# Output projection as a stage of its own, with the second norm's squares and sums between its columns

## The chip, the core and the metric

One Trainium2 chip, one core of it. The kernel is one program of 74 thousand instructions on five engines: TensorE (PE, with its weight loads shown apart as PEld), VectorE (DVE), ScalarE (ACT), GpSimd (POOL) and SyncE (SP, which issues the DMAs here). The metric is the device time of one execution in microseconds; lower is better. Runs of the same kernel differ by up to 4 us here.

## The reference

Two layers of a diffusion backbone over 640 tokens (512 latent, 128 context) of width 1024. What matters for the change is the middle of a layer:

```python
y, k_new, v_new, s_rwkv, s_lru = token_mixers(h, lp, ...)   # ends in concat([a, b, c]) @ lp['w_out']
x = x + g1 * y                                              # gated residual
h2 = rmsnorm(x, lp['norm2_g']) * (1.0 + sc2) + sh2          # x * rsqrt(mean(x*x) + eps) * g
x = x + g2 * peer_ffn(h2, ...)                              # begins with q = h2 @ peer_wq  (1024 x 2048)
```

So x has 1024 features for each token, and the second norm needs for each token the sum of 1024 squares of the x that the output projection has just updated.

## The kernel before

Features lie on the 128 partitions, tokens in the free dimension: `g.xT` is [128, 8, 640], eight chunks (KC = 8) of 128 features. All products are in float32 quality: an operand is split in a high and a low part of type float32r, and `split3` (L197 to L201) issues three matmuls for each product, of 320 columns each (half of the 640 tokens, so that a result of 640 tokens takes two PSUM banks).

`gemm` (L209) is one block that does a whole product of this kind; the output projection (8 output columns of 128 features, called "wout") and the query projection (16 columns, "query") are two calls of it. In it SP issues the weight chunks (512 KB each, a ring of R = 4), ACT rounds each to its high part (`high`, L242), DVE makes the low part (`low`, L293), PE runs a column of 2 halves x 8 chunks x 3 matmuls = 48 matmuls in one PSUM bank pair (R = 4 pairs, all eight banks), and DVE takes the sums. For wout, `take` is the gated residual in place on `g.xT` (L1538, three instructions: tokens 0 to 319, 320 to 511, 512 to 639). The first two columns (SR = 2) go chunk by chunk through the right-hand side, as its parts become ready; from then on a column is done at a time. High and low parts have two slots, so column n + 2 is rounded once column n is done.

A block begins and ends with a barrier of all engines; after wout there is also a block that clears the semaphores (`g.end`, L127). SP too issues nothing of the next block before that.

`norm_programs` (L435) gives a norm as parts that `gemm` puts ahead of its own work:

- `scalar_first`: ACT squares the eight chunks of xT (L448, 128x640 each).
- `tensor`: PE sums the squares over partitions, a matmul with an all-ones matrix in plain float32, for each chunk one of 512 and one of 128 columns (L471). The profile counts two instructions for each such float32 matmul (x32 for 16).
- `vector`: DVE turns the sums into mean plus epsilon (L476), then waits for the root, scales chunk by chunk (L486) and makes the low parts (L481).
- `scalar`: ACT computes the root as Ln (L453) and Exp (L455), each after a table load, then applies gain and shift (L460, two instructions for a chunk) and rounds to the high part (L465).

In the query block the order on each engine is thus:

- SP: `prefetch` (the keys `kt`, 1 MB; four chunks `u` of 512 KB), then the ring of four query weight chunks, then the rest as slots come free.
- ACT: squares 0 to 7, `high(0)`, `high(1)`, root, chunks of the norm, further `high`.
- PE: sums of the squares, then columns 0 and 1 chunk by chunk, then the rest.
- DVE: `low(0)`, `low(1)`, mean, (root), scaling and low parts of the norm, then takes and `low` in turn.

The same `norm_programs` serves the first norm of a layer and the final norm; for them the change leaves the order as it is. Everything from the end of the query block on (selection, gates, experts, fold) is later blocks that start one after the other.

Of the kernel before, what the change touches and what calls it, by code (L numbers as in the profile page):

```python
# [25 lines left out]
F32 = mybir.dt.float32  # L26
U32 = mybir.dt.uint32
F32R = mybir.dt.float32r
BF16 = mybir.dt.bfloat16
ALU = mybir.AluOpType  # L30
ACT = mybir.ActivationFunctionType
AX = mybir.AxisListType

P = 128
D = 1024
DEPTH = 2
NS = 512
NPR = 128
NT = NS + NPR
# [3 lines left out]
KC = D // P  # L43
# [13 lines left out]
RMS_EPS = 1e-6  # L57
# [139 lines left out]
def split3(pe, out, lhs, rhs, start=True, stop=True):  # L197

    pe.matmul(out, lhs[1], rhs[0], start=start, stop=False)  # L199
    pe.matmul(out, lhs[0], rhs[1], start=False, stop=False)  # L200
    return pe.matmul(out, lhs[0], rhs[0], start=False, stop=stop)  # L201
# [230 lines left out]
    c.then(ve.tensor_tensor(g.gain[:, i, :, :], g.gain[:, i, :, :], v(name).unsqueeze(2).broadcast_to([P, KC, 2]), ALU.mult))  # L432


def norm_programs(g, st, name, out, gain, shift, squares, low=None, kept=None, roots=None, chunks=None):  # L435

    nc = g.nc
    sq_ready, sum_ready, r_ready, steps = (g.sem(f"{name}_{x}") for x in ("squared", "summed", "root", "steps"))  # L440
    log_ready, scaled, normed, lowed = (g.sem(f"{name}_{x}") for x in ("log", "scaled", "normed", "low"))
    rs = g.sb(st, "rs", [P, 2, NT]) if roots is None else roots
    t = chunks
    raw = (lambda kc: out[:, kc, :]) if low is None else (lambda kc: t[:, kc % 3, :]) if kept is None else (lambda kc: kept[:, kc, :])

    def scalar_first(act):
        for kc in range(KC):
            nc.scalar.activation(squares[:, kc, :], g.xT[:, kc, :], ACT.Square).then_inc(sq_ready, 1)  # L448

    def scalar(act):  # L450
        act.wait_ge(steps, 1)

        nc.scalar.activation(rs[:, 1, :], rs[:, 0, :], ACT.Ln).then_inc(log_ready, 1)  # L453
        act.wait_ge(log_ready, 1)
        nc.scalar.activation(rs[:, 0, :], rs[:, 1, :], ACT.Exp, scale=-0.5).then_inc(r_ready, 1)  # L455

        for kc in range(KC):
            act.wait_ge(scaled, kc + 1)
            for c, (a, b) in enumerate(((0, NS), (NS, NT))):
                last = nc.scalar.activation(raw(kc)[:, a:b], raw(kc)[:, a:b], ACT.Identity,  # L460
                                            scale=gain(kc, c), bias=shift(kc, c) if shift else 0.0)
            last.then_inc(normed, 1)
            if low is not None:
                act.wait_ge(normed, 2 * kc + 1)
                nc.scalar.activation(out[:, kc, :], raw(kc), ACT.Copy).then_inc(normed, 1)  # L465

    def tensor(pe):
        for kc in range(KC):
            pe.wait_ge(sq_ready, kc + 1)
            for bank, (a, b) in enumerate(((0, NS), (NS, NT))):  # L470
                mm = pe.matmul(g.ps[:, bank, 0:b - a], g.ones, squares[:, kc, a:b], start=(kc == 0), stop=(kc == KC - 1))  # L471
            mm.then_inc(sum_ready, 1)
    def vector(ve):
        c = Counter(ve, steps)
        ve.wait_ge(sum_ready, KC)
        c.did(ve.tensor_scalar(rs[:, 0, :], g.flat[:, 0:NT], 1.0 / D, RMS_EPS, ALU.mult, ALU.add))  # L476
        ve.wait_ge(r_ready, 1)

        def lower(kc):
            ve.wait_ge(normed, 2 * kc + 2)  # L480
            ve.tensor_tensor(low[:, kc, :], raw(kc), out[:, kc, :].bitcast(F32), ALU.subtract).then_inc(lowed, 1)  # L481

        for kc in range(KC):
            if low is not None and kept is None and kc >= 3:
                ve.wait_ge(lowed, kc - 2)
            ve.tensor_tensor(raw(kc), g.xT[:, kc, :], rs[:, 0, :], ALU.mult).then_inc(scaled, 1)  # L486
            if low is not None and kc >= 1:
                lower(kc - 1)
        if low is not None:
            lower(KC - 1)  # L490

    return {"scalar_first": scalar_first, "scalar": scalar, "tensor": tensor, "vector_first": lambda ve: None, "vector": vector,
            "chunk_low": lowed}


# [1036 lines left out]
def residual_take(g, part):  # L1532

    def take(ve, oc, sums):
        for a, b in ((0, H2), (H2, NS), (NS, NT)):
            c, h = int(a >= NS), a // H2
            x = g.xT[:, bass.ds(oc, 1), a:b]
            i = ve.scalar_tensor_tensor(x, sums[:, h:h + 1, a - h * H2:b - h * H2], g.modT[:, bass.ds(part * KC + oc, 1), c], x,  # L1538
                                        ALU.mult, ALU.add)
        return i  # L1540
    return take


AHEAD = 64
IN_SELECT = 52
U_RING = 4
# [321 lines left out]
H2 = NT // 2  # L1868
# [479 lines left out]
def build(nc, dram):  # L2348
    ctx = ExitStack()
    with ctx:  # L2350
# [25 lines left out]
        with nc.Fori(0, DEPTH) as l:  # L2376
            g.begin()
            with ExitStack() as s1:
                g.proj = g.sb(s1, "proj", [P, NPROJ + 1, NT])
                g.vtok = g.sb(s1, "vtok", [P, TILES, VTOK])  # L2380
                with ExitStack() as s2:
                    g.h2 = [g.sb(s2, f"h{x}", [P, KC, NT], F32R) for x in ("hi", "lo")]
                    proj_stage(g, l)
                g.outT = g.sb(s1, "outT", [P, KC, NT])
                with ExitStack() as s2:
                    g.kctx = g.sb(s2, "kctx", [P, CB, PAST])
                    g.vctx = g.sb(s2, "vctx", [P, PAST // P, 512])
                    keep = (g.sb(s2, "ar", [P, 2, CA, TILES, 2, P]), g.sb(s2, "gt", [P, CA, NT]), g.sb(s2, "pc", [P, 2, CA, NT // CH]))
                    with ExitStack() as s3:
                        mod = Modulation(g, s3, lambda i: dram["mod_late"][l, i], g.modL, MODS_FIRST, 4)  # L2390
                        rwkv_prepare(g, l, keep, mod)
                    mix_stage(g, l, keep)
                    mix_finish(g, l, keep)
                with ExitStack() as s2:
                    out2 = [g.sb(s2, f"out{x}", [P, KC, NT], F32R) for x in ("hi", "lo")]
                    gemm(g, "wout", lambda oc: dram["w_out"][l, oc], KC, 4, 2, out2, residual_take(g, 2),
                         lambda st: split_programs(g, "out", g.outT, *out2))
            g.end()
            g.begin()
            with ExitStack() as s1:  # L2400
                h = g.sb(s1, "h", [P, KC, NT])
                hid = HiddenAhead(g, s1, l, h)
                own = Gathered(g, s1)
                with ExitStack() as s2:
                    sel = g.sb(s2, "sel", [P, 3, NT])
                    with ExitStack() as s3:
                        kt = g.sb(s3, "kt", [P, 2 * PH, P])
                        keys_loaded = g.sem("sel_keys_loaded")
                        qT = g.sb(s3, "qT", [P, 2 * PH, NT])

                        def prefetch(sync):
                            sync.dma_start(kt[:, :, :], dram["peer_keys"][l]).then_inc(keys_loaded, 16)
                            for n in range(U_RING):
                                hid.load(sync, n, n, first=True)

                        with ExitStack() as s4:
                            h2 = [g.sb(s4, f"h{x}", [P, KC, NT], F32R) for x in ("hi", "lo")]
                            gemm(g, "query", lambda oc: dram["peer_wq"][l, oc], 2 * PH, 4, 2, h2,
                                 lambda ve, oc, sums: ve.tensor_copy(qT[:, bass.ds(oc, 1), :].rearrange("p o (h n) -> p (o h) n", n=H2), sums),
                                 lambda st: norm_programs(g, st, "norm2", h2[0], lambda kc, c: g.gain[:, 1, kc, c:c + 1],  # L2420
                                                          lambda kc, c: g.modT[:, 3 * KC + kc, c:c + 1], h, low=h2[1], kept=h,
                                                          roots=sel[:, 0:2, :]), prefetch)
                        select_stage(g, l, qT, sel, kt, keys_loaded, hid, own)
                    gates_stored = [g.sem(f"gate_stored{i}") for i in range(2)]
                    gates_stage(g, l, sel, hid, gates_stored, own)
                experts_stage(g, l, hid, gates_stored, own)
                fold_stage(g, own.acc)
            g.end()

        g.begin()  # L2430
        with ExitStack() as s1:
            out = g.sb(s1, "out", [P, KC, NT])
            with ExitStack() as s2, nc.Block() as block:  # L2433
                final = norm_programs(g, s2, "final", out, lambda kc, c: g.v("final", kc, kc + 1), None, out)
                @block.scalar
                def _(act):
                    final["scalar_first"](act)
                    final["scalar"](act)
# [121 lines left out]
```

## Time and profile before

| | us |
|---|---|
| median of 3 runs | 4712.85 (4710.88 to 4714.87) |
| profiled execution | 4709.56 |
| its span | 4707.8 |
| PE busy | 4159.8 (88%) |
| DVE busy | 3554.3 (75%) |
| ACT busy | 1493.6 (32%) |

Engines are busy side by side, so the shares say little on one stage; a stage is read by which engine, wait or transfer ends last there. Each of the two layers has one wout block and one query block: wout from 747.5 to 817.0 us and from 3060.9 to 3130.4, query following from 818.25 and 3131.71. In a timeline a row is: start, length, engine, line, operation, output <- inputs, shape, count of merged instructions, and in brackets how long the engine idled before and what released it.

### The profile page before, as it was taken

Reading aid. Unit: us, or ns where it says so; the run is one execution under the profiler, and the core shown is the slowest. Engines: PE = TensorE matmul, PEld = TensorE weight load, DVE = VectorE, ACT = ScalarE, POOL = GpSimd, SP = SyncE. Lnnn points to the kernel's source line nnn. Section 1 sums busy time; section 2 is a strip of 40 time slices with the busy share of each in tenths; the row PEclk is TensorE's granted clock in tenths of the full one; section 3 lists DMA queues with packets and bytes.
Section 4 is the critical chain, followed back from the end, with each engine's and each line's share of the span. In section 5 each row is a group of like instructions: output and inputs, shape, how many; then the busy total and the mean of one; then the engine's idle time right before and its main releaser. Section 6 shows DMA issues by size and latency. Waiting matters only on the chain. (4 is left out here: it accounts for less than half of the span.)

```text
span 4707.8 us, 73952 instructions
## 1 busy us (share of the span) xinstructions
PE 4159.8 (88%) x28014; PEld 3384.9 (72%) x28014; DVE 3554.3 (75%) x6633; ACT 1493.6 (32%) x2210; POOL 1329.6 (28%) x1046
## 2 busy tenths in 40 slices
PE   7979987899698999999889799879987889999996
PEld 5957776865476887878779477579654678888875
DVE  3456643379997999999955566433899989999997
ACT  4424523211133333332252455231111332333333
POOL 0000000013303665666500000000332056566663
PEclk8978878999899999999999789789998999999998
DMA  6230002258779999999821300121786899999995
GB/s 234 63 115 2 2 2 105 85 182 308 258 205 326 409 409 408 404 406 404 331 90 41 115 2 2 56 98 52 274 287 204 242 388 409 409 405 407 403 406 222
DMA packets 408295, 1079.48 MB, mean 229 GB/s; under 512 B 37728, under 2 KB 183392, under 8 KB 401376
## 3 DMA queue, kind: packets, MB, share of 16 engines
q1 hardware_dynamic: 260576, 539.10, 32.3%
q0 software_dynamic: 147456, 536.94, 29.5%
q8 instruction: 157, 2.57, 0.2%
q14 instruction: 106, 0.87, 0.1%
HBM read 996.47 MB, written 79.43 MB: 229 GB/s over the span
## 5 line engine op out<-in xcount | busy, mean ns | idle before, releaser
L1618 POOL DMA_INDIRECT ring<-peer_u_rows,rows x512 | 625.7, 1222 | 2439.8 <-DVEq L1859 1512.8
L1618 POOL DMA_INDIRECT ring<-peer_v,rows x512 | 679.3, 1327 | 405.2 <-DVE acc L2252 336.1
L199 PE MATMUL ps<-vhi,wlo 128*128 128x512 f32 x1536 | 618.9, 403 | 134.8 <-DVE wlo L2231 133.1
L1575 PE MATMUL ps<-h,u 128*128 128x384 f32 x2048 | 689.0, 495 | 27.0 <-ACT hh L1586 25.0
L2252 DVE SCALAR_TENSOR_TENSOR acc<-ring,act,acc 128x1024 f32<-128x1024 f32 x508 | 647.3, 1281 | 45.8 <-DMA ring<-peer_v,rows 39.0
L1622 DVE SCALAR_TENSOR_TENSOR ring<-ring,acc 128x1024 f32<-128x1024 f32 x512 | 623.7, 1224 | 36.0 <-DMA ring<-peer_u_rows,rows 29.1
L200 PE MATMUL ps<-vlo,whi 128*128 128x512 f32 x1536 | 613.4, 399 | 0.0
L201 PE MATMUL ps<-vhi,whi 128*128 128x512 f32 x1536 | 612.9, 399 | 0.0
L1575 PEld LDWEIGHTS ps<-h,u 128*128 128x128 f32 x2048 | 390.2, 193 | 289.5 <-issue 42.9
L199 PEld LDWEIGHTS ps<-vhi,wlo 128*128 128x128 f32 x1536 | 297.7, 194 | 215.6 <-issue 142.0
L199 PE MATMUL ps<-xhi,ulo 128*128 128x384 f32 x1024 | 344.5, 336 | 18.6 <-DVE xlo L2209 18.6
L201 PE MATMUL ps<-xhi,uhi 128*128 128x384 f32 x1024 | 344.3, 336 | 0.0
L200 PE MATMUL ps<-xlo,uhi 128*128 128x384 f32 x1024 | 343.9, 336 | 0.0
L201 PEld LDWEIGHTS ps<-vhi,whi 128*128 128x128 f32 x1536 | 297.5, 194 | 64.3
L200 PEld LDWEIGHTS ps<-vlo,whi 128*128 128x128 f32 x1536 | 297.6, 194 | 61.5
L2217 DVE TENSOR_TENSOR vlo<-v,vhi 128x1024 fp32r<-128x1024 f32 x256 | 312.4, 1220 | 24.2 <-ACT vhi L2161 24.2
L2161 ACT ACTIVATE vhi<-v 128x1024 fp32r<-128x1024 f32 x256 | 269.6, 1053 | 169.2 <-DMA v<-peer_v 161.8
L2166 ACT ACTIVATE whi<-u 128x384 fp32r<-128x384 f32 x128 | 66.8, 523 | 682.8 <-DVE u L2226 682.8
L1586 ACT ACTIVATE hh<-ps 128x384 f32<-128x384 f32 x256 | 122.6, 481 | 424.0 <-PE ps L1575 391.5
L199 PE MATMUL ps<-hhi,proj_lo 128*128 128x320 f32 x672 | 210.5, 313 | 15.2 <-DVE hlo L481 15.2
L200 PE MATMUL ps<-hlo,proj_hi 128*128 128x320 f32 x672 | 208.8, 311 | 0.0
L199 PEld LDWEIGHTS ps<-xhi,ulo 128*128 128x128 f32 x1024 | 193.4, 189 | 21.4 <-DVE xlo L2209 19.0
(356 smaller groups left out, 8054.2 us busy)
## 6 DMA issues: line engine op xcount, KB each, us to landing
u<-peer_u SPq DMA_DIRECT2D x256, 512.0 KB
v<-peer_v SPq DMA_DIRECT2D x256, 512.0 KB
gates<-stage SPq DMA_DIRECT2D x24, 2048.0 KB, 9.6
gw<-gates SPq DMA_DIRECT2D x64, 768.0 KB
mod_ring<-mod_late SPq DMA_DIRECT2D x32, 1024.0 KB, 7.6
hidden<-hh SPq DMA_DIRECT2D x128, 192.0 KB
u<-hidden SPq DMA_DIRECT2D x128, 192.0 KB
proj_raw<-w_proj SPq DMA_DIRECT2D x42, 512.0 KB, 3.7
```

The source lines that it names most:

```text
L199: pe.matmul(out, lhs[1], rhs[0], start=start, stop=False)
L200: pe.matmul(out, lhs[0], rhs[1], start=False, stop=False)
L201: return pe.matmul(out, lhs[0], rhs[0], start=False, stop=stop)
L1575: mm = pe.matmul(self.g.ps[:, bank, 0:ND], self.u[:, slot, kc, :], self.x[:, kc, 0:ND], start=(kc == 0), stop=(kc == KC - 1))
L1586: return self.g.nc.scalar.activation(self.hh[:, slot, :], self.g.ps[:, slot, 0:ND], ACT.Gelu)
L1618: return pool.indirect_dma_start(to, None, table, rows)
L1622: return ve.scalar_tensor_tensor(row, row, 1.0, self.acc[:, x, :], ALU.mult, ALU.mult, accum_out=self.act[x][:, slot:slot + 1])
L2161: nc.scalar.activation(v2[0][:, j, :], v[:, j % 2, :], ACT.Copy).then_inc(v_hi, 1)
L2166: nc.scalar.activation(w2[0][:, j, :], h, ACT.Copy).then_inc(w_hi, 1)
L2217: ve.tensor_tensor(v2[1][:, j, :], v[:, j % 2, :], v2[0][:, j, :].bitcast(F32), ALU.subtract).then_inc(v_lo, 1)
L2252: ve.scalar_tensor_tensor(acc, r, w, acc, ALU.mult, ALU.add).then_inc(used, 1)
```

## The change

- `wout_stage` replaces the call of `gemm` for wout. It has the same columns, splits and residual, written out without loops: three PSUM bank pairs for the columns (`R`), banks 6 and 7 for the sums of squares. ACT squares a chunk of xT once DVE has updated it (`square`), behind the `high` of a later column, in a buffer of two chunks. PE sums the squares of column n - 2 behind column n (`squares`), those of columns 6 and 7 at the end.
- `norm_programs` takes `summed`, the place of finished sums in PSUM. With it, ACT squares nothing and PE sums nothing in the query block; DVE forms the mean as its first instruction (`vector_first`) and ACT the root as its first (`scalar_first`), both ahead of the query's weights.

```diff
-def norm_programs(g, st, name, out, gain, shift, squares, low=None, kept=None, roots=None, chunks=None):
+def norm_programs(g, st, name, out, gain, shift, squares, low=None, kept=None, roots=None, chunks=None, summed=None):
@@ -443,16 +443,22 @@
...
-    def scalar_first(act):
-        for kc in range(KC):
-            nc.scalar.activation(squares[:, kc, :], g.xT[:, kc, :], ACT.Square).then_inc(sq_ready, 1)
-
-    def scalar(act):
+    def root(act):
         act.wait_ge(steps, 1)
-
         nc.scalar.activation(rs[:, 1, :], rs[:, 0, :], ACT.Ln).then_inc(log_ready, 1)
         act.wait_ge(log_ready, 1)
         nc.scalar.activation(rs[:, 0, :], rs[:, 1, :], ACT.Exp, scale=-0.5).then_inc(r_ready, 1)
+    def scalar_first(act):
+        if summed is not None:
+            root(act)
+            return
+        for kc in range(KC):
+            nc.scalar.activation(squares[:, kc, :], g.xT[:, kc, :], ACT.Square).then_inc(sq_ready, 1)
+    def scalar(act):
+        if summed is None:
+            root(act)
...
     def tensor(pe):
-        for kc in range(KC):
+        for kc in range(KC) if summed is None else ():
             pe.wait_ge(sq_ready, kc + 1)
             for bank, (a, b) in enumerate(((0, NS), (NS, NT))):
                 mm = pe.matmul(g.ps[:, bank, 0:b - a], g.ones, squares[:, kc, a:b], start=(kc == 0), stop=(kc == KC - 1))
             mm.then_inc(sum_ready, 1)
+    def mean(ve):
+        at = 0 if summed is None else summed
+        ve.tensor_scalar(rs[:, 0, :], g.flat[:, at:at + NT], 1.0 / D, RMS_EPS, ALU.mult, ALU.add).then_inc(steps, 1)
     def vector(ve):
-        c = Counter(ve, steps)
-        ve.wait_ge(sum_ready, KC)
-        c.did(ve.tensor_scalar(rs[:, 0, :], g.flat[:, 0:NT], 1.0 / D, RMS_EPS, ALU.mult, ALU.add))
+        if summed is None:
+            ve.wait_ge(sum_ready, KC)
+            mean(ve)
         ve.wait_ge(r_ready, 1)
         def lower(kc):
@@ -489,7 +499,7 @@
         if low is not None:
             lower(KC - 1)
-    return {"scalar_first": scalar_first, "scalar": scalar, "tensor": tensor, "vector_first": lambda ve: None, "vector": vector,
+    return {"scalar_first": scalar_first, "scalar": scalar, "tensor": tensor, "vector_first": (lambda ve: None) if summed is None else mean, "vector": vector,
             "chunk_low": lowed}
@@ -1541,6 +1551,108 @@
     return take
+def wout_stage(g, l):
+    nc, d = g.nc, g.dram
+    R, S, W = 3, 2, 4
+    w_in = [g.sem(f"wout_w_loaded{i}") for i in range(W)]
+    w_hi, w_lo, ready, taken = (g.sem(f"wout_{x}") for x in ("w_high", "w_low", "sums_ready", "sums_taken"))
+    squared, summed = g.sem("norm2_squared"), g.sem("norm2_summed")
+    take = residual_take(g, 2)
+    with ExitStack() as st, nc.Block() as block:
+        out2 = [g.sb(st, f"out{x}", [P, KC, NT], F32R) for x in ("hi", "lo")]
+        parts = split_programs(g, "out", g.outT, *out2)
+        raw = g.sb(st, "wout_raw", [P, W, KC, P])
+        hi = g.sb(st, "wout_hi", [P, S, KC, P], F32R)
+        lo = g.sb(st, "wout_lo", [P, S, KC, P], F32R)
+        sq = g.sb(st, "sq", [P, 2, NT])
+        @block.sync
+        def _(sync):
+            for n in range(KC):
+                if n >= W:
+                    sync.wait_ge(w_lo, n - W + 1)
+                sync.dma_start(raw[:, n % W, :, :], d["w_out"][l, n]).then_inc(w_in[n % W], 16)
+        @block.scalar
+        def _(act):
+            def high(n):
+                act.wait_ge(w_in[n % W], 16 * (n // W + 1))
+                if n >= S:
+                    act.wait_ge(ready, n - S + 1)
+                nc.scalar.activation(hi[:, n % S, :, :], raw[:, n % W, :, :], ACT.Copy).then_inc(w_hi, 1)
+            def square(n):
+                act.wait_ge(taken, n + 1)
+                if n >= 2:
+                    act.wait_ge(summed, n - 1)
+                nc.scalar.activation(sq[:, n % 2, :], g.xT[:, n, :], ACT.Square).then_inc(squared, 1)
+            parts["scalar_first"](act)
+            for n in range(S):
+                high(n)
+            parts["scalar"](act)
+            for n in range(KC):
+                if n + S < KC:
+                    high(n + S)
+                if n >= 1:
+                    square(n - 1)
+            square(KC - 1)
+        @block.tensor
+        def _(pe):
+            def chunk(n, h, kc):
+                w = (hi[:, n % S, kc, :], lo[:, n % S, kc, :])
+                return split3(pe, g.ps[:, 2 * (n % R) + h, 0:H2], w, [x[:, kc, h * H2:(h + 1) * H2] for x in out2],
+                              start=(kc == 0), stop=(kc == KC - 1))
+            def squares(n):
+                pe.wait_ge(squared, n + 1)
+                for bank, (a, b) in enumerate(((0, NS), (NS, NT))):
+                    mm = pe.matmul(g.ps[:, 2 * R + bank, 0:b - a], g.ones, sq[:, n % 2, a:b], start=(n == 0), stop=(n == KC - 1))
+                mm.then_inc(summed, 1)
+            pe.wait_ge(w_lo, S)
+            for kc in range(KC):
+                pe.wait_ge(parts["chunk_low"], kc + 1)
+                for n in range(S):
+                    for h in range(2):
+                        mm = chunk(n, h, kc)
+                    if kc == KC - 1:
+                        mm.then_inc(ready, 1)
+            for n in range(S, KC):
+                pe.wait_ge(w_lo, n + 1)
+                if n >= R:
+                    pe.wait_ge(taken, n - R + 1)
+                for h in range(2):
+                    for kc in range(KC):
+                        mm = chunk(n, h, kc)
+                mm.then_inc(ready, 1)
+                squares(n - 2)
+            squares(KC - 2)
+            squares(KC - 1)
+        @block.vector
+        def _(ve):
+            def low(n):
+                ve.wait_ge(w_hi, n + 1)
+                ve.tensor_tensor(lo[:, n % S, :, :], raw[:, n % W, :, :], hi[:, n % S, :, :].bitcast(F32), ALU.subtract).then_inc(w_lo, 1)
+            parts["vector_first"](ve)
+            for n in range(S):
+                low(n)
+            parts["vector"](ve)
+            for n in range(KC):
+                ve.wait_ge(ready, n + 1)
+                take(ve, n, g.ps[:, 2 * (n % R):2 * (n % R) + 2, 0:H2]).then_inc(taken, 1)
+                if n + S < KC:
+                    low(n + S)
...
                     mix_finish(g, l, keep)
-                with ExitStack() as s2:
-                    out2 = [g.sb(s2, f"out{x}", [P, KC, NT], F32R) for x in ("hi", "lo")]
-                    gemm(g, "wout", lambda oc: dram["w_out"][l, oc], KC, 4, 2, out2, residual_take(g, 2),
-                         lambda st: split_programs(g, "out", g.outT, *out2))
+                wout_stage(g, l)
...
                                  lambda st: norm_programs(g, st, "norm2", h2[0], lambda kc, c: g.gain[:, 1, kc, c:c + 1],
                                                           lambda kc, c: g.modT[:, 3 * KC + kc, c:c + 1], h, low=h2[1], kept=h,
-                                                          roots=sel[:, 0:2, :]), prefetch)
+                                                          roots=sel[:, 0:2, :], summed=6 * 512), prefetch)
```

## Rows read from the trace of the kernel before

**Rows 1.** Busy time, share of the span and instructions of TensorE, from the page.
```profile
PE 4159.8 (88%) x28014; PEld 3384.9 (72%) x28014; DVE 3554.3 (75%) x6633; ACT 1493.6 (32%) x2210; POOL 1329.6 (28%) x1046
```

**Rows 2.** Timeline of DVE, layer 1, takes of wout columns 2, 3 and 7.
```profile
780.65 1.14 DVE L1538 SCALAR_TENSOR_TENSOR xT<-ps,modT,xT 128x320 f32<-128x320 f32 x3 [5.22 <-PE ps L201]
...
787.69 1.13 DVE L1538 SCALAR_TENSOR_TENSOR xT<-ps,modT,xT 128x320 f32<-128x320 f32 x3 [4.66 <-PE ps L201]
...
815.85 1.14 DVE L1538 SCALAR_TENSOR_TENSOR xT<-ps,modT,xT 128x320 f32<-128x320 f32 x3 [5.91 <-PE ps L201]
```

**Rows 3.** Group of one matmul form, 745 to 860 us: busy us, mean ns, idle before.
```profile
L199 PE MATMUL ps<-outhi,wout_lo 128*128 128x320 f32 x128 | 40.6, 317 | 11.4 <-DVE wout_lo L293 11.4
```

**Rows 4.** Timeline, layer 1: PE's sums of squares, then the query's first matmul.
```profile
819.04 8.92 PE L471 MATMUL ps<-h,keep 128*128 128x512 f32 x32 [3.23 <-ACT h L448]
819.57 0.19 PEld L471 LDWEIGHTS ps<-h,keep 128*128 128x128 f32 x1 [0.24 <-issue]
...
820.65 0.19 PEld L471 LDWEIGHTS ps<-h,keep 128*128 128x128 f32 x1 [0.24 <-issue]
...
840.57 0.60 PE L199 MATMUL ps<-hhi,query_lo 128*128 128x320 f32 x1 [12.61 <-DVE hlo L481]
```

**Rows 5.** Timeline of ACT, layer 1, query block up to the root.
```profile
818.25 5.12 ACT L448 ACTIVATE h<-xT 128x640 f32<-128x640 f32 x8 [15.36 <-PEq L127]
829.57 1.06 ACT L242 ACTIVATE query_hi<-query_raw 128x1024 fp32r<-128x1024 f32 x1 [6.20 <-DMA query_raw<-peer_wq]
830.84 1.06 ACT L242 ACTIVATE query_hi<-query_raw 128x1024 fp32r<-128x1024 f32 x1 [0.21 <-DMA query_raw<-peer_wq]
...
834.67 1.28 ACT L455 ACT_TABLE_LOAD   x1
```

**Rows 6.** Timeline of DVE, layer 1, query block up to the first scaling.
```profile
830.66 2.49 DVE L293 TENSOR_TENSOR query_lo<-query_raw,query_hi 128x1024 fp32r<-128x1024 f32 x2 [13.68 <-ACT query_hi L242]
833.07 0.81 DVE L476 TENSOR_SCALAR sel<-ps 128x640 f32<-128x640 f32 x1
836.74 1.56 DVE L486 TENSOR_TENSOR h<-xT,sel 128x640 f32<-128x640 f32 x2 [2.85 <-ACT sel L455]
```

**Rows 7.** Windows of 2 us in the query block, layer 1: PE, PEld, DVE, ACT, POOL busy, PEclk, DMA share, GB/s.
```profile
820.00:822.00 2.00, 2.00 (x9) 1.21 (x8) 0.00 (x0) 2.00 (x4) 0.00 (x0) 1.00 0.91 381
...
828.00:830.00 2.00, 0.00 (x0) 0.00 (x0) 0.00 (x0) 0.43 (x1) 0.00 (x0) 1.00 1.01 406
```

**Rows 8.** Timeline, layer 1, wout block: ACT's first work, PE's first matmul.
```profile
747.47 2.62 ACT L503 ACTIVATE outhi<-outT 128x640 fp32r<-128x640 f32 x4 [1.25 <-PEq L1453]
...
755.77 0.63 PE L199 MATMUL ps<-outhi,wout_lo 128*128 128x320 f32 x1 [9.76 <-DVE wout_lo L293]
```

**Rows 9.** Timeline of SP, layer 1: first DMA of wout, first of query.
```profile
747.84 28.15 SPq L232 DMA_DIRECT2D wout_raw<-w_out  x8
818.37 0.33 SPq L2412 DMA_DIRECT2D kt<-peer_keys  x1
```

**Rows 10.** Timeline, layer 2, all engines: squares, sums, first rounding, first scaling.
```profile
3131.71 5.12 ACT L448 ACTIVATE h<-xT 128x640 f32<-128x640 f32 x8 [15.36 <-PEq L127]
...
3132.49 11.84 PE L471 MATMUL ps<-h,keep 128*128 128x512 f32 x32 [3.23 <-ACT h L448]
...
3143.03 1.06 ACT L242 ACTIVATE query_hi<-query_raw 128x1024 fp32r<-128x1024 f32 x1 [6.20 <-DMA query_raw<-peer_wq]
...
3150.22 1.56 DVE L486 TENSOR_TENSOR h<-xT,sel 128x640 f32<-128x640 f32 x2 [2.85 <-ACT sel L455]
```

**Rows 11.** Windows around two entries of PE into a product; columns as in Rows 7.
```profile
757.00:759.00 2.00, 2.00 (x9) 2.00 (x9) 1.66 (x3) 0.00 (x0) 0.00 (x0) 0.50 0.79 215
759.00:761.00 2.00, 2.00 (x15) 2.00 (x13) 0.00 (x0) 0.00 (x0) 0.00 (x0) 0.91 0.17 68
842.00:844.00 2.00, 2.00 (x9) 2.00 (x9) 1.70 (x3) 1.97 (x5) 0.00 (x0) 0.50 0.00 0
844.00:846.00 2.00, 2.00 (x13) 2.00 (x12) 1.70 (x4) 1.97 (x4) 0.00 (x0) 0.83 0.03 8
```

## The prediction

> **What bounds the kernel now.** I read the page's busy shares first, then the groups of the stretch the diff touches, then its timelines engine by engine, then windows for DMA and the clock. PE is busy 88% of the span [rows 1], but that averages stages with other limits; the two edited blocks of a layer have to be read one by one.
>
> In the wout block PE is the limit. DVE takes column 2 at 780.65, column 3 at 787.69 and column 7 at 815.85 [rows 2]: 7.04 us from one to the next, five times over (35.20 / 5 = 7.04 to column 7). A column is 48 matmuls, so they follow each other every 0.147 us, and PE waits in this block only at its start and once behind the first two columns: 11.4 us in the group's idle time [rows 3], of which 9.8 us lie before the first matmul [rows 8] and 1.6 us are that second wait. DVE idles 4.66 us before a take, ACT more. Whatever is put on PE between columns lengthens this block; what is put on ACT or DVE does not.
>
> In the query block the limit, up to PE's first matmul at 840.57, is the load of the first weights. The block starts at 818.25; ACT's first rounding waits for the DMA until 829.57, the second until 830.84 [rows 5], 11.32 and 12.59 us after the start. In layer 2 the first comes at 3143.03 against 3131.71, again 11.32 [rows 10]. SP first issues keys and four u chunks; the DMA engines are at 0.91 of their time in a window while PE and ACT work and at 1.01 in one when both are idle [rows 7], so they carry what they can. The squares (5.12 us of ACT from 818.25, rows 5) and PE's sums (8.92 us from 819.04 to 827.96, rows 4) lie wholly beside this load and end 1.6 us before it. In layer 2 the sums took 11.84 us, to 3144.33 [rows 10], longer because PE ran a part of them at 1.2 GHz, and the scaling still began at the same distance from the block's start: 3150.22 - 3131.71 = 18.51, against 836.74 - 818.25 = 18.49 in layer 1. So the squares and the sums cost nothing today. What is exposed behind the load is the root: DVE makes the two low parts from 830.66, then the mean at 833.07, and scales from 836.74 [rows 6]. Mean, Ln, a table load and Exp are the 3.67 us between.
>
> **The change, part by part**, per layer, against the profiled execution (4709.56 us; the median of the runs is 3.3 above it).
>
> *Root first: a gain of 3.67 us.* The mean, the root and both table loads move to the block's start, on DVE and ACT, which have nothing else until 829.57. They are a 0.81 us mean, two loads of 1.28 us and two activations, some 5 us in all, under 11 us of load; that cover holds with 6 us to spare. DVE then scales where the mean stood, at 833.07 instead of 836.74 on the old time axis. ACT is free by then (its second rounding ends at 831.90). The norm's chunks follow at ACT's rhythm as before.
>
> The next sentences are by the way. In the trace the table load between Ln and Exp lasted 1.28 us and Exp came right behind it [rows 5]. The Trainium skill (ScalarE: Activation LUTs, "What ACT_TABLE_LOAD costs") puts a switch at 2.66 us, of which 1.38 are a drain. By it the exposed root would be 3.67 + 1.38 = 5.05 us and the net loss below 1.4 us smaller per layer. The timeline has no room for that drain, so the row decides.
>
> *Squares to ACT in wout: nothing.* Eight activations of 0.64 to 0.74 us (5.12 / 8 and one with its tail, rows 5), each behind a `high`, in a stage where ACT works about 1 us in 7. Only the last one is on the path, below. A square waits for the take of its column; the `high` queued behind it waits for a later column anyway, so nothing is held up.
>
> *Sums to PE between columns: a loss.* The weight loads of the sums repeat every 820.65 - 819.57 = 1.08 us for one chunk of 640 tokens at full clock [rows 4]. Five of them (chunks 0 to 4, behind columns 2 to 6) stand before the end of column 7. PE's other waits there are unchanged: the 1.6 us wait comes before column 2, the first sum only after it. So the last take starts at 815.85 + 5 x 1.08 = 821.25.
>
> *The new tail.* Before, the block's last work was the take, to 816.99. Now behind column 7, which ends for PE at about 821.05, come two more sums, to 823.21. Meanwhile the take ends at 822.39 and ACT's last square, 0.74 us and a handover, at 823.18. Then the last sum: 8.92 - 7 x 1.08 = 1.36 us with its drain, to 824.57. The block ends 824.57 - 816.99 = 7.6 us later. SP issues the query's loads only behind the barrier, so the whole 7.6 shifts the landing at 829.57 too. The bounds of this term: no more than 0 if PE had hidden waits for the sums; the price of a sum is 1.08 us at full clock and twice that at 1.2 GHz ((11.84 - 8.92) = 2.9 us more in layer 2), which I exclude because 0.147 us for a matmul is the high clock: at 1.2 GHz PE started only 9 in 2 us [rows 11]. What the trace doesn't show is a plain float32 matmul between float32r ones. From below it could overlap by the 0.15 us of one matmul; from above it could cost a fill on both sides, some 0.3 us by the 0.60 us of PE's first matmul against a mean of 0.317 [rows 3, 4]. I take 0, as PE goes through the sums' own switches between 512 and 128 columns without a gap.
>
> *Loops gone: a gain of 0.2 us.* SP's first DMA of wout comes 0.37 us after ACT's first work [rows 8, 9], that of the query, which has no loop ahead, 0.12 us after it [rows 5, 9]. The first weights gate PE's start, so 0.25 at most, 0 at least.
>
> *Clock.* PE enters wout and query at 0.50, 1.2 GHz, and leaves it within 3 to 5 us [rows 11]. It idled 9.8 and 12.6 us ahead of them [rows 4, 8]. After the change it will idle some 20 us ahead of the query and enter at the same level. Only how long it stays there may vary: 1.5 us more or less of low clock is 0.75 us per entry.
>
> *The sum*: +7.6 - 3.67 - 0.2 = +3.7 us per layer, +7.4 in both. Behind the query block everything starts in sequence and shifts along. Profiled: 4717.0 us. Runs: 4712.85 + 7.4 = 4720.3.
>
> **Rivals.**
>
> *Sums that cost more than their own time (slower).* Each is a switch of operand type, twice, in PE's stream. 16 sums carry it. My sum passes +0.2% (+9.4 us, about what a measurement here can tell from no change) once the extra is over (9.4 - 7.4) / 16 = 0.13 us each. At the upper bound of 0.3 us it is +4.8: 4725. A barrier that takes longer when PE's matmul is last, and low clock at the wrong place, add to the same side. For it: no row shows such a mixture. Against: no gap in PE's own sums.
>
> *Sums that are free (the norm's front simply shortens).* If PE had room between columns, only the tail would be left: behind the take's end a square and the last sum, 0.79 + 1.36 = +2.1, and -3.67 - 0.2, so -1.8 per layer, 4709.3. For it: the group's 11.4 us idle of PE [rows 3]. Against: none of them lies behind column 2's start, and the takes are evenly 7.04 apart.
>
> *The load is faster once nobody else works.* Squares and sums read SBUF during the load. Were the landing 2 us earlier, each layer would gain 2: 4716, and with free sums 4705. Against: 0.91 with PE and ACT at work, 1.01 without; and layer 2 landed after the same 11.32 us with sums 2.9 us longer.
>
> **How the numbers follow.** My case, with each term inside its bounds: 0.62, 4716 to 4722. Costlier sums or barrier: 0.25, above 4722.3, mostly below 4728. Free sums: 0.08, around 4709. Faster load: 0.05. Only the last two together go below 4703.4, 0.04 of it all. So faster 0.04, slower 0.25, within 0.2% 0.71. The range 4715.5 to 4727.5 leaves out the free sums and a little at the top.
>
> **What would show it.** Takes of columns 3 to 7 spaced 8.12 us instead of 7.04; the wout block 7.6 us longer from its first work to the next block's; no L448 and L471 in the query block; the first rounding still 11.3 us behind its start, the scaling 14.8 instead of 18.5; PE's first query matmul at 18.6 instead of 22.3 us. It would be wrong if takes are 7.1 or over 8.3 us apart, or if the first rounding comes at another distance.

## Result and profile after

| | before | after |
|---|---|---|
| median of 20 runs each | 4712.52 us | 4722.52 us (4712.21 to 4731.24) |
| ratio, 95% interval | | 1.0020 [1.0014, 1.0026] |
| the same pair once more (35 and 12 runs) | 4713.32 us | 4718.27 us, 1.0012 [1.0002, 1.0021] |
| span of the profiled execution | 4707.8 us | 4729.4 us |

The forecast was 4720.3 us. The first pair came out 10.0 us slower, the second 5.0; the forecast was 7.4. The two profiled executions lie 21.6 us apart, most of it (15.2 us) in a stage that the change doesn't touch, so the trace has to be read by stretches.

DVE in layer 1, the takes of columns 2, 3 and 7 and then its first work of the query block, answers to [rows 2, 6]:

```profile
788.86 1.14 DVE L1548 SCALAR_TENSOR_TENSOR xT<-ps,modT,xT 128x320 f32<-128x320 f32 x3 [5.22 <-PE ps L201]
...
796.98 1.14 DVE L1548 SCALAR_TENSOR_TENSOR xT<-ps,modT,xT 128x320 f32<-128x320 f32 x3 [5.75 <-PE ps L201]
...
829.46 1.14 DVE L1548 SCALAR_TENSOR_TENSOR xT<-ps,modT,xT 128x320 f32<-128x320 f32 x3 [6.99 <-PE ps L201]
834.08 0.82 DVE L481 TENSOR_SCALAR sel<-ps 128x640 f32<-128x640 f32 x1 [3.49 <-PEq L127]
846.73 2.50 DVE L293 TENSOR_TENSOR query_lo<-query_raw,query_hi 128x1024 fp32r<-128x1024 f32 x2 [11.82 <-ACT query_hi L242]
849.14 1.55 DVE L496 TENSOR_TENSOR h<-xT,sel 128x640 f32<-128x640 f32 x2
```

The takes are 8.12 us apart instead of 7.04, in layer 2 as well. The mean stands alone at the block's start, and the scaling follows the low parts at once, without the 2.85 us wait of [rows 6]. The end of the output projection, all engines (weight loads left out):

```profile
829.26 3.50 PE L1616 MATMUL ps<-sq,keep 128*128 128x512 f32 x12
829.46 1.14 DVE L1548 SCALAR_TENSOR_TENSOR xT<-ps,modT,xT 128x320 f32<-128x320 f32 x3 [6.99 <-PE ps L201]
...
830.63 0.74 ACT L1593 ACTIVATE sq<-xT 128x640 f32<-128x640 f32 x1 [7.38 <-DVE xT L1548]
...
834.02 1.28 ACT L448 ACT_TABLE_LOAD   x1 [2.65 <-PEq L127]
```

The last three sums run to 832.76, 3.30 us behind the start of the last take. ACT begins the next block 1.26 us later, as long as the barrier took behind the take before (816.99 to 818.25). ACT's part of the query block, answers to [rows 5]:

```profile
835.31 0.74 ACT L448 ACTIVATE sel<-sel 128x640 f32<-128x640 f32 x1
836.07 1.28 ACT L450 ACT_TABLE_LOAD   x1
837.36 0.74 ACT L450 ACTIVATE sel<-sel 128x640 f32<-128x640 f32 x1
845.64 1.06 ACT L242 ACTIVATE query_hi<-query_raw 128x1024 fp32r<-128x1024 f32 x1 [7.54 <-DMA query_raw<-peer_wq]
```

The root is done at 838.10, and ACT then waits 7.54 us for the weights. They land 11.5 us behind SP's first DMA of the block (834.16) in this layer and 11.3 in the other; before it was 11.2.

From such rows, by the first work of each stretch (us; M is the mixing stage ahead, from the store of the new keys to the output projection; "edited" runs from ACT's first work in the output projection to the query's first take, DVE's `qT` copy):

| kernel | M, layer 1 / 2 | edited, layer 1 / 2 | edited, sum against before (217.4) | median against before |
|---|---|---|---|---|
| before | 418.0 / 421.0 | 108.5 / 108.9 | | |
| before, again | 426.9 / 427.3 | 109.0 / 108.3 | | -0.3 |
| after | 427.9 / 426.3 | 111.7 / 112.7 | +7.1 | +10.0 |
| after, again | 420.8 / 421.0 | 112.5 / 112.6 | +7.7 | +5.0 |
| stage only | 424.6 / 424.3 | 108.8 / 108.7 | +0.1 | +0.5 |
| one sum | 427.5 / 420.8 | 107.6 / 108.5 | -1.3 | -0.9 |
| before, weights first | 428.2 / 416.7 | 103.4 / 106.1 | -7.8 | -4.4 |
| after, weights first | 417.9 / 420.5 | 104.9 / 104.9 | -7.5 | -4.7 |
| three sums | 420.4 / 419.8 | 107.8 / 106.8 | -2.8 | -4.1 |
| four sums, weights first | 427.4 / 421.3 | 104.3 / 103.6 | -9.4 | -4.9 |

(217.4 is the mean of the two profiles of the kernel before. Medians are against that of the kernel before in runs taken alongside: 4712.52 for the first row of after, 4713.32 down to "one sum", 4711.52 for the last four.)

What is left of the span beside M and the edited stretches takes 3648 to 3653 us in all ten profiles, without an order by kernel. From the query's first take to the end of the query block it is 102.3 us in both layers of every one. So what an edited stretch loses or gains isn't taken back later.

### The profile page after: what moved, and what is told of

Its sections match the earlier page's. It is cut to its first block and busy times, and to the rows that moved or that the text cites. A ratio compares the mean times of both kernels' runs of the same rounds, so it can differ in the third digit from the quotient of the medians.

```text
span 4729.4 us, 73908 instructions
## 1 busy us (share of the span) xinstructions
PE 4166.3 (88%) x28014; PEld 3397.1 (72%) x28014; DVE 3552.9 (75%) x6633; ACT 1494.3 (32%) x2210; POOL 1318.4 (28%) x1046
## 5 line engine op out<-in xcount | busy, mean ns | idle before, releaser
L1730 POOL DMA_INDIRECT ring<-peer_v,rows x512 | 660.5, 1290 | 424.0 <-DVE acc L2364 365.2
L199 PE MATMUL ps<-xhi,ulo 128*128 128x384 f32 x1024 | 344.4, 336 | 18.6 <-DVE xlo L2321 18.6
L199 PE MATMUL ps<-hhi,proj_lo 128*128 128x320 f32 x672 | 211.3, 314 | 16.3 <-DVE hlo L491 16.3
L201 PE MATMUL ps<-hhi,proj_hi 128*128 128x320 f32 x672 | 209.4, 312 | 0.0
```

The costliest lines, as they stand in the source:

```text
L1730: return pool.indirect_dma_start(to, None, table, rows)
```

## Experiments

**The same two kernels again.** No edit.

> The changed kernel once more, unaltered, for a second profile and more times. My theory: the change costs 3.2 to 3.8 us per layer in the two edited blocks (output projection 6.9 to 7.5 us longer from ACT's first work to the next block's first DMA, query 3.7 to 3.8 shorter up to its first take), 7 us in all, and the rest of the 10 us between the medians is the spread of the mixing stage, whose clock is uneven. It expects the same two differences again (70.9 to 78 us; 37.6 to 34 us), and the mixing stage of either layer anywhere from 416 to 430 us. Rival: the changed program makes the mixing stage itself slower. It expects 426 us or more again in both layers, against 418 and 421 before.

> The kernel before once more, unaltered, for a second profile of it. My theory (the mixing stage's time varies by itself): the mixing stage differs from 418.0 and 421.0 us by some us in either direction in at least one layer, the two edited blocks by less than 0.5 us (70.9 and 37.6). Rival (the changed program makes it slower): 418 to 421 us again in both layers. Ratio to the kernel before 1.000.

Measured: 4718.27 us (ratio 1.0012 [1.0002, 1.0021]) and 4713.07 us (0.9994 [0.9984, 1.0003]). Windows over M in the second profile of before and in the second of after, each layer a row (columns as in Rows 7):

```profile
329.50:756.40 426.90, 370.32 (x4905) 285.00 (x4904) 257.99 (x537) 175.63 (x370) 0.00 (x0) 0.80 0.06 23
2647.70:3075.00 427.30, 369.93 (x4904) 284.69 (x4896) 258.07 (x537) 175.54 (x370) 0.00 (x0) 0.80 0.07 23
```

```profile
329.60:750.40 420.80, 364.94 (x4908) 279.48 (x4907) 257.93 (x537) 175.18 (x371) 0.00 (x0) 0.81 0.07 23
2646.80:3067.70 420.90, 362.29 (x4908) 277.35 (x4907) 258.01 (x537) 175.34 (x370) 0.00 (x0) 0.82 0.07 23
```

With the same work of DVE and ACT, M takes 417 to 428 us in the ten profiles: the stretches over 426 us all have a mean granted clock of 0.80, the 416.7 of the kernel before with weights first has 0.83. PE runs the same matmuls in more busy time at the lower clock (370.32 against 364.94 and 362.29 us above). The rival (the changed program slows M) is out: before has it at 427 twice, after at 421 twice. The edited stretches repeat to within 0.8 us in a layer: in the second profile of the changed kernel the output projection takes 78.3 and 78.4 us, the query 34.3 and 34.2 to its first take.

**The stage alone, without squares.**

```diff
-    roots=sel[:, 0:2, :], summed=6 * 512), prefetch)
+    roots=sel[:, 0:2, :]), prefetch)
...
-                if n >= 1:
-                    square(n - 1)
-            square(KC - 1)
...
-                squares(n - 2)
-            squares(KC - 2)
-            squares(KC - 1)
```

> The output projection as a stage of its own without loops, with three pairs of banks, but without any square or sum in it; the second norm squares and sums in the query block as before, and its root stands behind the weights as before. My theory: only the loop's start goes, so the output projection takes 70.2 to 70.7 us instead of 70.9, query stays at 37.6 us to its first take, and the total is 0.4 to 1.4 us below the kernel before (4711 to 4712 if that is at 4712.5). Rival (the new stage itself, its written-out code or fewer banks, costs time): output projection over 71.5 us or total over 4716.

Measured: 4713.85 us, 1.0001 [0.9990, 1.0011]; the output projection takes 70.7 us in both layers (before: 70.9 twice, then 71.0 and 70.5), the query 38.0 us to its first take. The total didn't fall by the expected 0.4 to 1.4 us; a gain of that size can't be seen in these medians. SP's first DMA now stands 0.10 us behind ACT's first work instead of 0.36, but what that saves up to the end of the block is within the spread of the kernel before. Writing it out without loops and with three bank pairs costs nothing, and the rival (over 71.5 us) is out.

**All sums but one left out.**

```diff
             def squares(n):
                 pe.wait_ge(squared, n + 1)
+                if n < KC - 1:
+                    pe.sem_inc(summed, 1)
+                    return
...
-                    mm = pe.matmul(g.ps[:, 2 * R + bank, 0:b - a], g.ones, sq[:, n % 2, a:b], start=(n == 0), stop=(n == KC - 1))
+                    mm = pe.matmul(g.ps[:, 2 * R + bank, 0:b - a], g.ones, sq[:, n % 2, a:b], start=True, stop=True)
```

> The changed kernel with the sums of squares of chunks 0 to 6 left out (only chunk 7 is summed, so the second norm's root is another number); all squares, waits and the rest stay. My theory (each sum costs PE its own 1.08 us, nothing hides it): the takes of columns 3 to 7 are 7.04 us apart again instead of 8.12, the output projection takes 70.2 to 71 us instead of 77.8 and 78.4, and the total falls by 14 to 15.5 us against the changed kernel, to about 4707.5. Rival (sums cost more than their own time): it falls by 18 us or more. Rival (sums were free, the loss lies elsewhere): it falls by less than 5 us.

Measured: 4712.42 us, 5.9 below the changed kernel on the same chip, its edited stretches 9.1 us shorter; expected were 14 to 15.5. DVE's takes of columns 6 and 7, ACT's last square and PE's one sum:

```profile
816.85 1.13 DVE L1548 SCALAR_TENSOR_TENSOR xT<-ps,modT,xT 128x320 f32<-128x320 f32 x3 [4.66 <-PE ps L201]
823.89 1.14 DVE L1548 SCALAR_TENSOR_TENSOR xT<-ps,modT,xT 128x320 f32<-128x320 f32 x3 [5.91 <-PE ps L201]
```

```profile
825.06 0.74 ACT L1593 ACTIVATE sq<-xT 128x640 f32<-128x640 f32 x1 [6.30 <-DVE xT L1548]
...
825.85 1.35 PE L1619 MATMUL ps<-sq,keep 128*128 128x512 f32 x4 [2.00 <-ACT sq L1593]
```

The takes are 7.04 us apart again, as expected. But the output projection took 72.7 and 73.6 us, not 70.2 to 71. My expectation was wrong by two sums: those of chunks 5 and 6, behind column 7, run beside the last take and square. The tail from the last take's start to the end of the last sum is 823.89 to 827.20, 3.31 us, against 3.30 with those two sums in place. So of eight sums five are paid for in full (5 x 1.08 = 5.4 us), two are free, and of the last the whole length is a tail. Neither rival holds: the stretches shrank by far less than 18 us and by more than 5, though the median by only 0.9 us more than 5; that sums aren't free rests on the takes.

The query's part up to its first take was 34.8 us in both layers, 0.6 to 0.9 us longer than in the changed kernel. Windows from PE's first query matmul to that take, here and in the first profile of the changed kernel (columns as in Rows 7):

```profile
847.45:863.43 15.98, 15.98 (x93) 15.98 (x94) 10.04 (x13) 11.93 (x21) 0.00 (x0) 0.83 0.01 3
3161.07:3177.32 16.25, 16.25 (x93) 16.25 (x94) 10.05 (x14) 11.91 (x21) 0.00 (x0) 0.82 0.01 3
```

```profile
852.97:868.13 15.16, 15.16 (x93) 15.16 (x94) 10.04 (x13) 11.93 (x21) 0.00 (x0) 0.88 0.01 2
3176.36:3192.03 15.67, 15.67 (x93) 15.67 (x94) 10.04 (x14) 11.92 (x21) 0.00 (x0) 0.85 0.02 6
```

The extra time lies in this part, at a lower granted clock. Why PE stays at 1.2 GHz longer here isn't shown. The mean granted clock of the timed runs of this kernel is lower too, 0.917 against 0.920 in those of the kernel before and the changed one, and it computes with other numbers, so its median says less than its stretches.

**Weights first.** The same edit of `gemm` in the kernel before and in the changed one:

```diff
+            for j in range(R):
+                sync.dma_start(raw[:, j, :, :], weights(j)).then_inc(w_in[j], 16)
             if prefetch is not None:
                 prefetch(sync)
-            with sync.Fori(0, n_out // R) as i:
+            with sync.Fori(0, n_out // R - 1) as i:
                 for j in range(R):
-                    sync.wait_ge(w_lo, i * R + (j + 1))
-                    sync.dma_start(raw[:, j, :, :], weights(i * R + j)).then_inc(w_in[j], 16)
+                    sync.wait_ge(w_lo, i * R + (j + 1 + R))
+                    sync.dma_start(raw[:, j, :, :], weights(i * R + (j + R))).then_inc(w_in[j], 16)
```

> The kernel before, but SP issues the first four query weight chunks ahead of the keys and the u chunks. My theory (in the kernel before, the first weights' landing 11.2 us behind the block's start hides squares and sums): with weights early, the sums are exposed instead: they end 9.7 us into the block (12.6 where PE runs a part at 1.2 GHz), and mean, Ln, load and Exp follow, so DVE scales at 13.4 us (16.2) instead of 18.5. The stretch from the block's first DMA to its first take falls from 37.6 to 32.5 us in layer 1 and 38 to 33 to 36 in layer 2, output projection stays at 70.9, the total falls by 5 to 10 us (4703 to 4708). Rival (weights do not set the time, the norm's own work does): the stretch stays at 37 us or more.

> The changed kernel with the same new order of loads. My theory: the sums are already paid for in the output projection and the root ends 4.1 us into the block, so the weights alone set the time: first rounding 3.7 us behind the first DMA instead of 11.4, DVE scales at some 7.4 us instead of 15.1, first take at 26.6 us instead of 34. Output projection stays at 78. Total 14 to 16 us below the changed kernel, 5 to 10 below the kernel before. Rival (the DMA engines need the same time whatever comes first): first rounding over 7 us behind the first DMA.

Measured: 4707.12 us (0.9989 [0.9980, 0.9997]) and 4706.81 us (0.9989 [0.9980, 0.9998]), the second's edited stretches some 15 us below those of the changed kernel (-7.5 against +7.1 and +7.7). Against the kernel before the medians fell by 4.4 and 4.7 us, a little less than the expected 5 to 10, while the stretches fell by 7.8 and 7.5. From the first DMA to the first take it was 33.3 and 35.3 us in the kernel before (expected 32.5, and 33 to 36) and 26.8 in the changed one (expected 26.6). Layer 1 of the kernel before with weights first, ACT and then DVE:

```profile
827.86 5.12 ACT L450 ACTIVATE h<-xT 128x640 f32<-128x640 f32 x8 [15.36 <-PEq L127]
832.89 1.99 ACT L244 ACTIVATE query_hi<-query_raw 128x1024 fp32r<-128x1024 f32 x2
...
838.46 0.74 ACT L455 ACTIVATE sel<-sel 128x640 f32<-128x640 f32 x1 [2.29 <-DVE sel L478]
```

```profile
837.60 0.82 DVE L478 TENSOR_SCALAR sel<-ps 128x640 f32<-128x640 f32 x1 [1.28 <-PE ps L473]
841.28 0.82 DVE L488 TENSOR_TENSOR h<-xT,sel 128x640 f32<-128x640 f32 x1 [2.85 <-ACT sel L457]
```

The weights are there as soon as ACT is done squaring, and the mean now waits for PE's sums: scaling at 841.28 - 827.86 = 13.4 us, as expected. In layer 2, where PE ran a part of the sums at 1.2 GHz, the stretch is 106.1 us instead of 103.4. Layer 1 of the changed kernel with weights first, ACT and then DVE:

```profile
824.83 1.28 ACT L450 ACT_TABLE_LOAD   x1 [2.65 <-PEq L127]
...
828.17 0.74 ACT L452 ACTIVATE sel<-sel 128x640 f32<-128x640 f32 x1
828.82 2.23 ACT L244 ACTIVATE query_hi<-query_raw 128x1024 fp32r<-128x1024 f32 x2
```

```profile
832.22 1.55 DVE L498 TENSOR_TENSOR h<-xT,sel 128x640 f32<-128x640 f32 x2
```

Scaling at 7.4 us. The root is done at 828.91, 3.9 us behind the first DMA (824.98), and that is when the weights land (3.92 us in the last experiment, where ACT waits for them). So the root isn't exposed here, and what its new place and the missing sums gain pays for the sums in the output projection: the two kernels are equal. Both rivals (the norm's own work or the DMA engines' total sets the time) fall: the stretch is under 37 us, and the first rounding stands 4.9 and 3.8 us behind the first DMA, not over 7.

**Three sums early.** Chunks 0 to 2 in the output projection, 3 to 7 at the query block's start, into the same banks; then mean and root, still ahead of the weights.

```diff
-                squares(n - 2)
-            squares(KC - 2)
-            squares(KC - 1)
+                if n - 2 < 2:
+                    squares(n - 2)
+            squares(2)
...
     def scalar_first(act):
-        if summed is not None:
-            root(act)
-            return
-        for kc in range(KC):
+        for kc in range(done, KC):
             nc.scalar.activation(squares[:, kc, :], g.xT[:, kc, :], ACT.Square).then_inc(sq_ready, 1)
+        if summed is not None:
+            root(act)
...
```

> The changed kernel with only chunks 0 to 2 squared and summed in the output projection (sums 0 and 1 behind columns 2 and 3, sum 2 behind column 7 beside the last take); chunks 3 to 7 are squared and summed at the start of the query block, under the load of the weights, and mean and root come next, still ahead of the weights. My theory: two sums are paid for, the tail is free, so the output projection takes 72.4 to 73 us instead of 78; sums, mean and root end some 10 us into the query block (13 if PE is at 1.2 GHz), so its first take stays at 34 us (up to 36). Each layer 1 to 2 us below the kernel before, the total 4708 to 4711. Rival (a sum costs PE more than its time wherever it stands between other products, or the tail is longer than I think): output projection 74 us or more.

Measured: 4707.43 us, 0.9987 [0.9978, 0.9995], a little under the expected 4708 to 4711; output projection 72.7 and 73.1 us, edited stretches 2.8 us below before, where 2 to 4 were expected. The rival (74 us or more) is out. PE's sums in its query block, layer 1:

```profile
823.11 7.37 PE L476 MATMUL ps<-h,keep 128*128 128x512 f32 x20 [2.15 <-ACT h L454]
```

At 1.08 us each and 0.28 for the drain five would take 5.7 us: PE was partly at 1.2 GHz, and they still ended (830.48) before the weights' landing. The root ended at 834.16 and the first rounding went at once behind it, 11.6 us after the first DMA: 0.1 to 0.4 us behind the landing of the kernels in which ACT waits for it (11.2 to 11.5 us). DVE scales 15.1 us behind the block's start, as in the changed kernel, though ACT squares and PE sums five chunks in this block again. So what the query block gains comes from the root's place and not from the squares and sums that are gone from it, and it is a net gain once most sums stay where they are free.

**Both.** Four sums early, root behind the first roundings, and `gemm` with weights first.

```diff
-                squares(n - 2)
-            squares(KC - 2)
-            squares(KC - 1)
+                if n - 2 < 3:
+                    squares(n - 2)
+            squares(3)
...
     def scalar(act):
-        if summed is None:
-            root(act)
+        root(act)
...
```

> Both ideas together: chunks 0 to 3 are squared and summed in the output projection (three sums paid for, the fourth beside the last take), chunks 4 to 7 at the start of the query block, the root behind the first two roundings as in the kernel before, and the first four weight chunks ahead of keys and u chunks. My theory: output projection 73.5 us, sums done 5.4 to 6.2 us into the block, root ends at 10.1 us, first take at 29 to 30 us (up to 33 where PE runs the sums at 1.2 GHz): 5 to 6 us per layer below the kernel before, total 4701 to 4704, the best of all. Rival (the two ideas meet in the same gap and do not add): not below the better of the two kernels with weights first.

Measured: 4706.67 us, 0.9990 [0.9979, 1.0000], not the expected 4701 to 4704. The output projection took 74.0 and 73.4 us (expected 73.5), the first take came 30.3 and 30.2 us behind the first DMA (29 to 30). ACT's first rounding in layer 1, where SP's first DMA stands at 830.78:

```profile
834.70 1.06 ACT L244 ACTIVATE query_hi<-query_raw 128x1024 fp32r<-128x1024 f32 x1 [1.43 <-DMA query_raw<-peer_wq]
```

Issued first, the weights land after 3.92 us instead of 11.2. By the stretches this kernel is the best (-9.4 us), by the median it can't be told from the other two with weights first, so the rival isn't excluded by the times; its profile had M at 427.4 in layer 1. That it beats the kernel before is shown by its stretches, not by its interval, which touches 1.

## Why the prediction was right

*PE is the limit of the output projection, a sum costs its own 1.08 us.* Right to the hundredth: takes at 8.12 instead of 7.04 us, five times over in each layer, and back at 7.04 without the sums. The unknown of the trace before, a float32 matmul between float32r ones, costs nothing beyond that; the rival that priced it at 0.3 us is out.

*The tail.* Forecast 3.3 us from the last take's start to the last sum's end, measured 3.30. The barrier behind a matmul is no longer than behind a take (1.26 us both). Together, over two profiles each, the output projection went from 70.8 to 78.2 us: +7.4, as +7.6 and -0.2 had said.

*Root first gains 3.67 us.* From the block's first DMA to the first take it is 37.7 before and 34.0 us after in layer 1, 38.0 and 34.3 in layer 2; the means of two profiles each are 37.8 and 34.2. That it is the root's place, three sums early shows. The table load between Ln and Exp took 1.28 us again, and Exp started 1.29 us behind the load's start (836.07 to 837.36). So the longer switch that the Trainium skill gives (ScalarE: Activation LUTs, "What ACT_TABLE_LOAD costs") isn't seen here either.

*The landing sets the query block.* The first rounding stood 11.5 and 11.3 us behind the first DMA, 11.2 before, though nobody squared or summed beside it: the rival of the faster load is out. Counted from ACT's first work it is 11.3 to 11.6 us in the two profiles where 11.3 was forecast, so scaling came at 14.8 to 15.1 (forecast 14.8) and PE's first query matmul at 18.7 to 19.0 (18.6). Weights first shows the cause of the late landing, the 3 MB of keys and u chunks ahead of them.

*Loops gone.* Forecast 0.2. SP starts 0.26 us earlier against ACT, as the rows had said; in the length of the block 0.2 us can't be told from the spread.

*Free sums*, the rival at 4709, is out by the takes alone. (By its own terms, 0.79 + 1.36 - 3.67 - 0.2, it is -1.7 per layer and not -1.8.)

*The sum.* +3.7 us per layer were forecast; the two profiles show +3.0 to +4.1, together 7.1 and 7.7 in both layers against the forecast 7.4. So the mechanism and its size were right.

The first median, 4722.52, is another matter. By the forecast's own bins it lies just above "my case" (4716 to 4722) and in that of costlier sums or barrier, which the traces rule out; the second, 4718.27, lies in "my case". The first being inside the range of 4715.5 to 4727.5 owes something to the part of that range that was there for the rival.

The rest of the 10.0 us of the first median, and what the second (5.0) lacks, fits the spread of the mixing stage. The timed runs show no stages, but each has a mean granted clock. Over the 35 runs of the kernel before, the time falls as that clock rises (correlation -0.75, some 2.7 us for each 0.001). The changed kernel's first 20 runs have 0.9186 on average, its second 12 have 0.9197. By that slope 3 of the 4.3 us between its two medians go with the clock, as an estimate. In which stage of the timed runs that lies isn't shown.

What the forecast lacked was that spread: I had called run-to-run differences 4 us from three runs, where 35 runs of the kernel before lay between 4704 and 4722.

## What to carry over

Before work is moved out of a stage, ask what hides it there: squares and sums looked like 9 us of the norm's front and cost nothing, because a load of 11 us ran beside them; between the columns of a full PE the same sums cost their whole length. If a load is the cover, ask next whether the load must be that long: issuing the first needed weights ahead of a 3 MB prefetch took 8 us off the edited stretches of both layers before the change and 15 us after it. Where an untouched stage varies by more than the change is worth, compare the edited stretches of two profiles and use medians only as a bound.

## What was not expected of the hardware

The mixing stage takes 416.7 to 428.2 us for the same instructions, in either layer, at mean granted clocks of 0.80 to 0.83. Within the stage PE's granted clock goes between 1.2 and 2.4 GHz at moments that differ from run to run: from 380.5 to 392 us it is 1.00 in the first profile of the kernel before and 0.50 in the second, 51 us behind the stage's start in both.

Plain float32 and float32r matmuls follow each other without a gap: the first of the sums behind column 7 starts 0.15 us behind the last float32r matmul (829.11 and 829.26), as these do behind each other.

PE at the query block's start runs its sums sometimes at 2.4 GHz throughout (8.92 us) and sometimes at 1.2 GHz for a part (11.84 us, [rows 10]) behind the same 3.2 us pause. From its first query matmul to the first take it needs 14.9 us (mean granted clock 0.90) to 16.3 us (0.82), both seen in one profile of the kernel with three sums early.
